# Second input projection: ten gate and query tiles as five pairs of seven half-size products, the third weight sum of pairs two to five on GpSimd

## What is computed

```python
h = _rms(x, norm_g) * (1.0 + scale) + shift
u = h @ w_in                       # 1024 x 1984
cq     = u[..., 0:256]             # query latent: 2 tiles of 128 columns
ckv    = u[..., 256:384]           # key/value latent: 1 tile
k_rope = u[..., 384:448]           # rotary keys: 1 tile, half used
gate_a = u[..., 448:960]           # gate of the attention branch: 4 tiles
pool_in = u[..., 960:1472]         # input of the pooling branch: 4 tiles
gate_p = u[..., 1472:1984]         # gate of the pooling branch: 4 tiles
q = (_rms(cq, q_lora_g) @ w_uq)
pooled = window_mean(pool_in) - pool_in        # windows 2, 4, 8, 16 of four groups
y_p = (pooled @ w_pool[group]) * pool_scale
br_a = silu(gate_a) * attention(q, k, v)
br_p = silu(gate_p) * y_p
out = x + gate * (concat(br_a, br_p) @ w_out)
```

## Time and profile before

| | us |
|---|---|
| median of 3 runs | 1904.95 |
| lowest and highest | 1904.12, 1905.85 |
| span of the profiled execution, from its first to its last instruction | 1904.2 |
| TensorE busy | 1864.6 |
| VectorE busy | 1397.6 |
| GpSimd busy | 906.7 |
| ScalarE busy | 733.7 |

### The profile page before, as it was taken

One profiled execution on the slowest core, in us unless ns is written; L12 is line 12 of the kernel. 1 busy time (PEld: TensorE's weight loads), 2 busy tenths in 40 slices (PEclk: granted clock), 3 DMA queues, 4 the chain that ended last, 5 costly groups with the idle time before them and its releaser, 6 DMA issues.

```text
span 1904.2 us, 23795 instructions
## 1 busy us (share of the span) xinstructions
PE 1864.6 (98%) x8807; PEld 1544.8 (81%) x8807; DVE 1397.6 (73%) x1423; ACT 733.7 (39%) x990; POOL 906.7 (48%) x632
## 2 busy tenths in 40 slices
PE   7999999999999999999999999999999999999998
PEld 6788888778888888888887788878788878888887
DVE  7989988667348889898989786574633846667683
ACT  5433344441225333333341200243433236766643
POOL 5866766533334555555566555332233521222462
PEclk9999999999999999999999999999999999999999
DMA  4112234356112323232336435111123210000052
GB/s 164 52 45 89 67 111 144 122 177 187 45 45 66 100 67 99 66 99 66 99 136 232 146 106 198 56 41 38 45 82 112 84 45 1 12 12 1 1 177 67
DMA packets 190952, 166.63 MB, mean 88 GB/s; under 512 B 11267, under 2 KB 168912, under 8 KB 190864
## 3 DMA queue, kind: packets, MB, share of 16 engines
q1 hardware_dynamic: 189536, 162.82, 27.0%
q10 hardware_dynamic: 1328, 2.60, 0.4%
HBM read 134.72 MB, written 30.41 MB: 87 GB/s over the span
## 4 chain that ended last, share of the span: by engine, by line
PE 84%; DVE 8%; ACT 3%; issue 2%; DMA 1%; POOL 1%; ACTq 0%; SPq 0%; DVEq 0%
PE ps L963 33%; PE ps L1251 19%; PE ps L1108 16%; PE ps L1638 3%; PE ps L1454 2%; PE ps L1489 1%; PE ps L1487 1%; PE ps L1488 1%; PE ps L1468 1%; PE ps L1465 1%; PE ps L1471 1%; PE ps L1474 1%; PE ps L1462 1%; DVE resid L2707 1%; DVE mod_acc L2410 1%
## 5 line engine op out<-in xcount | busy, mean ns | idle before, releaser
L833 POOL TENSOR_TENSOR small<-ones 128x1 f32<-128x1 f32 x75 | 22.2, 296 | 479.0 <-PE ps L963 438.7
L963 PE MATMUL ps<-xb_hi,whi 128*128 128x512 f32 x752 | 244.6, 393 | 5.1 <-DVE resid L2707 2.3
L963 PE MATMUL ps<-xb_lo,whi 128*128 128x512 f32 x752 | 242.2, 389 | 0.0
L963 PE MATMUL ps<-xb_hi,wlo 128*128 128x512 f32 x752 | 242.0, 389 | 0.0
L838 POOL TENSOR_TENSOR wlo<-raw,whi 128x1024 fp32r<-128x1024 f32 (+1 forms) x72 | 197.4, 2742 | 6.0
L879 POOL TENSOR_TENSOR wlo<-w_sums,whi 128x512 fp32r<-128x512 f32 x80 | 138.1, 1745 | 82.3 <-ACT whi L1956 82.3
L963 PEld LDWEIGHTS ps<-xb_hi,whi 128*128 128x128 f32 x752 | 140.2, 188 | 38.0 <-DVE resid L2707 3.1
L963 PEld LDWEIGHTS ps<-xb_lo,whi 128*128 128x128 f32 x752 | 141.2, 188 | 29.7 <-issue 0.2
L963 PEld LDWEIGHTS ps<-xb_hi,wlo 128*128 128x128 f32 x752 | 141.2, 188 | 29.6
L2390 DVE SCALAR_TENSOR_TENSOR ps<-glu_pad,tab,ps 128x1024 f32<-128x1024 f32 x116 | 149.2, 1286 | 2.9
L933 POOL TENSOR_SCALAR prob<-prob,small 128x512 f32<-128x512 f32 x64 | 50.5, 802 | 180.8 <-DVE small L3045 180.2
(11 more groups left out here) (493 smaller groups left out, 4824.6 us busy)
## 6 DMA issues: line engine op xcount, KB each, us to landing
t<-in_w_mod SPq DMA_DIRECT2D x48, 256.0 KB, 2.9
f_scratch<-t SPq DMA_DIRECT2D x22, 512.0 KB, 2.7
raw<-in_w_down SPq DMA_DIRECT2D x22, 512.0 KB, 4.2
raw<-in_w_up SPq DMA_DIRECT2D x40, 256.0 KB, 3.7
w_raw<-in_w_up SPq DMA_DIRECT2D x40, 256.0 KB, 3.7
raw<-in_w_in SPq DMA_DIRECT2D x18, 512.0 KB, 4.0
raw<-in_w_in SPq DMA_DIRECT2D x36, 256.0 KB, 4.0
w_in_raw<-in_w_in SPq DMA_DIRECT2D x32, 256.0 KB, 3.7
```

What stands on the lines that cost most here:

```text
L833: nc.gpsimd.tensor_tensor(small[:, 106 + slab.slot:107 + slab.slot], ones[:, 0:1], ones[:, 0:1], ALU.mult)
L963: ins = mm(dst[j], w, r[j], start=first and f, stop=last and l)
```

## The change

The ten tiles become five pairs (`UP_AT`, `u_product`): pair 0 the query tiles, 1 and 2 gate_a, 3 and 4 gate_p. The four combinations of h are made by four in-place subtractions on VectorE from a second, full copy of h (`hfull`, written by ScalarE beside the high part), then split in high (`comb_hi`) and low (`comb_low`). GpSimd makes the weight low halves and, for pairs 1 to 4, the third weight sum. The four pooling tiles now come right after the key tiles, the row sums stand in the first of them before k step 3, and the first two products with w_pool follow the second and third pooling tile, the other two stand between products of pair 0. Pooled outputs and Silu gates go through DRAM and come back for the products of gate and pooled output (`branch_gate`) and, before the first head's result, as `ga`. In the heads two branch tiles are split in place of one.

```diff
+NUP = 5
+UP_AT = {(0, 1): 0}
+for _p in range(NUP):
+    for _k in (2, 6, 5, 7):
+        UP_AT[_p, _k] = len(UP_AT)
+    if _p + 1 < NUP:
+        UP_AT[_p + 1, 1] = len(UP_AT)
+    for _k in (4, 3):
+        UP_AT[_p, _k] = len(UP_AT)
+UP_PRODUCTS = len(UP_AT)
...
+                for g in range(UP_PRODUCTS):
+                    slot, cols = u_ring(g)
+                    pool.wait_ge(*on("u_hi", g + 1))
+                    nc.gpsimd.tensor_tensor(wlo[:, slot, cols], u_source(*UP_OF[g]), f32(whi[:, slot, cols]),
+                                            ALU.subtract).then_inc(sem("u_split"), 1)
+                    p, k = UP_OF[g]
+                    if k == 3 and p + 1 < NUP:
+                        u_raw_in(pool, p + 1)
+                        pool.wait_ge(*on("u_split", g + 1))
+                        nc.gpsimd.tensor_tensor(u_sum(p + 1, 2), u_raw(p + 1, 0), u_raw(p + 1, 2), ALU.subtract).then_inc(sem("u_third"), 1)
+                pool.wait_ge(*on("u_done", UP_AT[4, 7] + 1))
                 head_split(0)
+                pool.wait_ge(*on("u_done", UP_PRODUCTS))
...
-        gemm(J + 4, L + 2, XBh, XBl, KD, w8)
-        gemm(J + 5, L + 3, XBh, XBl, KD, w8)
-
         def lora_sums(n):
 
-            if n == 2:
+            if n == 3:
                 pe.wait_ge(sem("y_ready"), 8)
                 row_sums(sqck, NKEY, sem("lora_sq"), 3)
...
+        def pooled_product(n):
+
+            gq = GROUPS[n]
+            pe.wait_ge(split_done, SLABS["w_pool"] + 2)
             pe.wait_ge(sem("branch2_lo"), n + 1)
-            gemm(J + (2 * n + 1), None, XAh[:, 4 + gq:5 + gq, :], XAl[:, 4 + gq:5 + gq, :], 1,
-                 lambda k: (gq, slice(0, P)), new_slab=False, weights=(wpoolh, wpooll))
+            if n:
+                pe.wait_ge(*on("wp_read", n))
+            else:
+                pe.wait_ge(sem("ck_f"), 1)
+            halves = [(PS[:, H * (6 + c):H * (7 + c)], slice(H * c, H * (c + 1))) for c in range(2)]
+            split_products([o for o, _ in halves], wpoolh[:, gq, :], wpooll[:, gq, :], [plh[:, 0, q] for _, q in halves],
+                           [pll[:, 0, q] for _, q in halves], True, True).then_inc(sem("wp_done"), 1)
+
+        J = Lin(JOBS["pin"])
+        L, LB = Lin(SLABS["pin"]), Lin(SLABS["pin_b"])
+        gemm(J, L, XBh, XBl, KD, w8, between=lora_sums)
+        gemm(J + 1, L + 1, XBh, XBl, KD, w8, begins=3)
+        pooled_product(0)
+        gemm(J + 2, LB, XBh, XBl, KD, w8)
+        pooled_product(1)
+        gemm(J + 3, LB + 1, XBh, XBl, KD, w8)
+
+        def u_product(p, k):
+
+            g, o = UP_AT[p, k], win_bank(p, k)
+            slot, cols = u_ring(g)
+            pe.wait_ge(*on("u_split", g + 1))
+            if p == 0 and k in HX:
+                pe.wait_ge(*on("hx_dve", 4 + HX_ORDER.index(k) + 1))
+            if (p, k) == (0, 5):
+                pe.wait_ge(pair_free[1], (J + 3).half() + 1)
+            if (p, k) == (1, 1):
+                pe.wait_ge(pair_free[0], (J + 2).half() + 1)
+            if k == 1 and p >= 2:
+                pe.wait_ge(*on("u_act", 3 * p - 5))
+            if k == 2 and p >= 2:
+                pe.wait_ge(*on("u_add", 3 * p - 5))
+            if k == 5 and p >= 2:
+                pe.wait_ge(*on("u_add", 3 * p - 3))
+            if k in (6, 7, 4):
+                pe.wait_ge(*on("u_copy", 3 * p + {6: 1, 7: 2, 4: 3}[k]))
+            if k == 3:
+                pe.wait_ge(*on("u_add", 3 * p + 2))
+            for j in range(4):
+                w = slice(cols.start + j * P, cols.start + (j + 1) * P)
+                if k in HX:
+                    b, k0, c0 = HX[k]
+                    bh, bl = xch[:, b, j, :], XAl[:, k0 + j, c0:c0 + H]
+                else:
+                    k0, c0 = {1: (0, 0), 2: (4, 0), 3: (4, H)}[k]
+                    bh, bl = XBh[:, k0 + j, c0:c0 + H], XBl[:, k0 + j, c0:c0 + H]
+                for i, (wp, bp) in enumerate(((whi, bh), (whi, bl), (wlo, bh))):
+                    last = mm(o, wp[:, slot, w], bp, start=k in (1, 2, 5) and j == 0 and i == 0,
+                              stop=j == 3 and i == 2, skip_group_check=True)
+            last.then_inc(sem("u_done"), 1)
+
+        for p, k in UP_AT:
+            u_product(p, k)
+            if (p, k) == (0, 1):
+                pooled_product(2)
+            if (p, k) == (0, 5):
+                pooled_product(3)
+            if (p, k) == (1, 7):
+                pe.wait_ge(*on("wp_read", 4))
+                column_sums(pres[0], 8, 16, sem("s12_done"), 23)
 
...
             fn(XBh[:, m, :], hT[:, m, :], ACT.Identity, bias=mod_sb[:, m, 0:1]).then_inc(sem("h_hi"), 1)
-        row_log(Q1, D, 6, 0, S, at_col=6 * H)
-        row_scale(PS[:, 6 * H:6 * H + S], Q1[:, :]).then_inc(sem("rbc_ready"), 1)
+            fn(hfull[:, m, :], hT[:, m, :], ACT.Identity, bias=mod_sb[:, m, 0:1]).then_inc(sem("h_hi"), 1)
+        row_log(rbc, D, 6, 0, S, at_col=6 * H)
+        row_scale(PS[:, 6 * H:6 * H + S], rbc[:, :]).then_inc(sem("rbc_ready"), 1)
+
+        def comb_hi(k):
+
+            b, k0, c0 = HX[k]
+            act.wait_ge(*on("hx_dve", HX_ORDER.index(k) + 1))
+            fn(xch[:, b, :, :], hfull[:, k0:k0 + 4, c0:c0 + H], ACT.Copy).then_inc(sem("hx_hi"), 1)
+
+        for k in HX_ORDER[:3]:
+            comb_hi(k)
         keys_out(J + 2, 0, S)
         rope_out(J + 3, 0, S)
...
+        def u_hi(g):
+
+            if g >= UP_PRODUCTS:
+                return
+            p, k = UP_OF[g]
+            slot, cols = u_ring(g)
...
+                act.wait_ge(*on("u_done", g - 1 if g == UP_PRODUCTS - 2 else g - 3))
+            if k in (1, 2, 4):
+                u_raw_in(act, p)
+            elif k == 7 and p:
+                act.wait_ge(sem("u_third"), p)
+            else:
+                act.wait_ge(*on("u_sum", up_sums(p, k)))
+            fn(whi[:, slot, cols], u_source(p, k), ACT.Copy).then_inc(sem("u_hi"), 1)
+
+        def u_copy(p, n):
+
+            k, to = ((1, upc[p % 2][:, 0:H]), (6, upc[p % 2][:, H:S]), (7, upd[p % 2][:, H:S]))[n]
...
+            act.wait_ge(*on("u_done", UP_AT[p, k] + 1))
+            fn(to, win_bank(p, k), ACT.Copy).then_inc(sem("u_copy"), 1)
...
+        def branch_high(p, n):
+
+            act.wait_ge(*on("u_dve", 2 * (p - 3) + n + 1))
+            act.wait_ge(*on("u_done", UP_AT[4, 5] + 1))
+            fn(XAh[:, 4 + GATE_P[p][1 - n], :], (upd, upc)[n][p % 2][:, :], ACT.Copy).then_inc(sem("branch2_hi"), 1)
...
+            if p == 0:
+                pooled_out(3)
+                comb_hi(4)
+            u_hi(b + 7)
+            if p + 1 < NUP:
+                u_copy(p + 1, 0)
+                u_hi(b + 8)
+                u_hi(b + 9)
+            else:
+                branch_high(3, 0)
+                branch_high(3, 1)
+            u_last_block(p)
+            u_hi(b + 10)
+            u_finish(p)
...
             if m >= 1:
-                dve.wait_ge(sem("h_hi"), m)
+                dve.wait_ge(sem("h_hi"), 2 * m)
                 dve.wait_ge(sem("h_n"), m)
                 stt(XBl[:, m - 1, :], hT[:, m - 1, :], mod_sb[:, m - 1, 0:1], f32(XBh[:, m - 1, :]),
                     ALU.add, ALU.subtract).then_inc(sem("h_lo"), 1)
-        dve.wait_ge(sem("lora_sq"), 6)
-        tt(cqs[:, 0, :], cqs[:, 0, :], cqs[:, 1, :], ALU.add).then_inc(sem("s12_done"), 1)
+        dve.wait_ge(sem("h_hi"), 16)
+        for n, (to, a, b) in enumerate((((0, 0), (0, H), (0, 0)), ((0, H), (4, H), (0, H)), ((4, H), (4, H), (0, 0)), ((4, 0), (4, 0), (4, H)))):
+            o, x, y = (hfull[:, k0:k0 + 4, c0:c0 + H] for k0, c0 in (to, a, b))
+            if n:
+                dve.wait_ge(*on("hx_dve", n))
+            tt(o, x, y, ALU.subtract).then_inc(sem("hx_dve"), 1)
         dve.wait_ge(sem("rbc_ready"), 5)
         for m in range(8):
             stt(R[:, m, :], R[:, m, :], col("g_final", m), PS[:, 6 * H:6 * H + S], ALU.mult, ALU.mult).then_inc(sem("y_ready"), 1)
 
+        def comb_low(k):
+
+            b, k0, c0 = HX[k]
+            dve.wait_ge(*on("hx_hi", HX_ORDER.index(k) + 1))
+            tt(XAl[:, k0:k0 + 4, c0:c0 + H], hfull[:, k0:k0 + 4, c0:c0 + H], f32(xch[:, b, :, :]), ALU.subtract).then_inc(sem("hx_dve"), 1)
+
+        for k in HX_ORDER[:3]:
+            comb_low(k)
         nc.vector.tensor_copy(onesr[:, :], ones[:, :]).then_inc(sem("ksq_ready"), 1)
-        dve.wait_ge(sem("ksq_hi"), 1)
-        tt(KSQ[ROPE:P, :], sqkr[:, :], f32(KSQ[0:ROPE, :]), ALU.subtract).then_inc(sem("ksq_ready"), 1)
         J = Lin(JOBS["mla_in"])
         dve.wait_ge(sem("y_out"), GOES_ON["y_out"][1] + 8 * 16)
-        for k in range(2):
...
+        for x in (upad, wA, wB):
+            nc.vector.memset(x[:, :], 0.0).then_inc(sem("pads2_zero"), 1)
         dve.wait_ge(*free(J + 3))
         dve.wait_ge(sem("rope_in"), 96)
-        tt(U3[0:ROPE, 0:S], U3[0:ROPE, 0:S], sinb[:, :], ALU.mult).then_inc(sem("krot_mul"), 1)
-        tt(krot[:, 0:S], krT[:, 0:S], cosb[:, :], ALU.mult).then_inc(sem("krot_done"), 1)
```

(8 more changed lines are left out.)

409 lines of the change are left out of this document (274 added, 135 removed).

## The result

The median of four runs is 1931.9 us (1930.6 to 1935.1) against 1905.4 us for the kernel before in the same session: 1.0140 times as long, 95% interval 1.0126 to 1.0155. The profiled execution took 1932.6 us, its span is 1930.8 us, 26.6 more than the span of the kernel before. The forecast was 1929 us, from a span 24.2 us longer.

The account below looks back on a forecast made before the run. TensorE, busy 98% of the span, was taken as the bound. Savings of 13.6 and 0.9 us against new waits, clock loss and other costs summed to +24.2 on 1904.2, 1928.4 in span, 1929 us as median; range 1916 to 1937.

Parts of the forecast that it names:

- What bounds, what is removed: Rewritten stretch: TensorE bounds, half-size products cost the same per matmul; 60 fewer give -13.6 us, the gate's Silu wait -0.9.
- Entry: Up to the end of the key tiles: double writing of h delays VectorE's low parts and TensorE, +1.1 us.
- First wait: First pooling tile: TensorE waits for VectorE's differences and g_final products before the row sums, +12.5 us; slab split, +1.4.
- Second wait: First pooled product, after the second pooling tile: TensorE waits for VectorE's low part of that group, +12.7 us.
- Pairs: Half-size products in steady state: GpSimd and ScalarE work hides, moved third sums cost 0; two places do not hide.
- Fourth combination: After product 7 of pair one: h's fourth combination is made late, so TensorE waits, +3.8 us.
- Last pair: End of the pairs: no next pair's product to put between, so bank copies are waited for, +2.0 us.
- Clock: Behind the waits: lower granted clock counts only after the second wait, +1.7 us.
- Head entry: First head: the last pair's final sum and Silu come first, two branch tiles are split, TensorE waits, +3.5 us.
- Rival 1: VectorE is ready when TensorE comes, at both waits and the fourth combination: 1897 us, faster; chance 0.06.
- Rival 2: Only the wait ahead of the row sums occurs, as pooling catches up: 1915 us; chance 0.12.
- Rival 3: More collisions of VectorE and GpSimd: 1937 us; chance 0.13.

Follow-up runs that it names:

- experiment 5: Changed kernel with the third weight sum of pairs two to five moved from GpSimd back to VectorE: 1931.7 us, ratio 1.0144.
- Experiment 1: Changed kernel with the row sums of the key latent moved from the first pooling tile to the second: 1931.1 us, ratio 1.0136.
- Experiments 1 to 4: Changed kernel with row sums a tile later (1931.1 us), g_final products ahead of three differences (1925.8), low parts behind pooled groups (1932.2), both of the last two (1920.2).
- experiment 6: Changed kernel with ScalarE making the high part of h's fourth combination before reading the last pooled output: 1928.2 us, ratio 1.0124.
- experiment 10: Changed kernel with many reorderings, pooled groups in order of one to four shifts: 1909.5 us; the same without the last group's four shifted adds: 1902.3 us.
- experiment 7: Changed kernel with two ScalarE steps reordered, latent-key high parts before rotary ones and product 6's copy before a weight half: 1929.3 us, ratio 1.0128.
- experiment 2: Changed kernel with g_final products after the first difference of h and ScalarE's latent and rotary key copies before the combinations' high parts: 1925.8 us, ratio 1.0107.

## Why the prediction was right, and where only its sum was

**What bounds, what is removed.** Right: half-size products cost the same per matmul. The 84 matmuls of a pair take 19.04 us (1524.11 to 1543.15, experiment 5), 0.2267 each.

**Entry**, +1.1: measured +0.9. VectorE's last low part, with the 0.7 us of the common part taken off, ended at 1388.3, 1.0 earlier than the 1389.3 of the sum.

**First wait**, 13.9 with the split: 9.4 measured. The first piece, 5.1 in place of 1.4, had a second cause that the sum lacked: the slab's low half came 3.5 us behind TensorE, not 1.4, and ScalarE's copy out of the bank, behind three high parts, 1.6 later still. That only divides the stop; its end is VectorE's eighth product with g_final, as the sum said. The step that was mis-sized is "four differences end at 1403.3". They met one GpSimd low half and not two, so that the eighth product came 21.6 us behind the last low part, not 23.6. Of the 4.5 that the term was too high this is 2.0; 0.9 are TensorE's later arrival, 6.5 us behind the last low part and not 5.6, and 1.5 are matmuls at the lower clock, which took what would else be wait. Experiment 1 shows that this size did not matter for the sum as long as the second stop comes behind it.

**Second wait**, +12.7: measured +13.4. Experiments 1 to 4 show that it is the whole list that ends there, with the store of y as a second bound at its middle, both of which the sum had. The length of the list, 56.0 us in the sum and 56.7 measured, owes something to luck, since two errors cancel: up to the eighth product it was 2.0 shorter than forecast, and behind it 2.7 longer (35.1 against 32.4). The store landed 1.0 later, the rotary steps took 1.0 more, the first shifted add beside GpSimd's split 2.0 more (3.27 us against 1.25), and the low part of the rotary squares was done 1.5 sooner.

**Pairs.** The moved third sum cost nothing (experiment 5), though for another reason than the rows that the sum read: beside it none of VectorE's sums was stretched. Fourth combination 3.8, measured 3.7; experiment 6 took off the 1.5 us of the steps put ahead of it. Last pair 2.0, measured 2.1.

**Clock**, +1.7: measured +7.6. I charged the lower clock once, behind the second wait. By TensorE's starts it cost 1.5 us behind the first stop (18 matmuls from 1400.52 to 1406.14, 5.6 us where 4.1 are due), 1.8 behind the row sums' stop, 2.7 behind the pooled product's (14 matmuls from 1445.67 to 1451.56, 5.9 for 3.2) and 1.5 behind the fourth combination's. The first two are paid by nobody: they make the next wait shorter by as much, as the prediction said of the first, and so they are missing from the two waits' measured sizes (10.9 and 15.2 with them, 26.1 together, where the sum had 26.6). What I left out is 1.0 behind the pooled product and 1.5 behind the fourth combination. The step that was mis-sized is "+1.7": in this execution a stop of 3.7 us brought the clock down too.

**Head entry**, +3.5: measured +3.4, and 349.8 to 351.7 us from the head to the end in the other traces, so 3.2 to 5.1.

**Rivals.** Rival 1 (VectorE hidden after all) is out by both waits; even in the version of experiment 10 that computes everything TensorE still stands 5.2 us for a low part of VectorE. Rival 2 (only the first wait) is out: the second was the longer one. Rival 3 (1937) stays outside the runs, 1930.6 to 1935.1.

## What to carry to other kernels

Where one engine works through a list and another meets it at several points, the waits must not be priced one by one: find the last point at which they meet, and ask how long the list is up to there and how much the other engine can do before it. A saving of matmuls that is paid for with element-wise steps on VectorE is worth nothing where VectorE has no time left: here 13.6 us of TensorE against eight steps of 2.3 us on VectorE, for the combinations of h alone. Beside a list, look for the second bound that lies just under it (the store of y), since it decides whether a single edit shows anything.

## What was not expected of the hardware

Behind every stop of TensorE of 3.7 to 13.4 us in the changed kernel matmuls ran at the lower granted clock, 0.50, for some 2.7 to 5.4 us, 7.6 us of time in all, while the kernel before, with 1.0 us idle in the stretch, has none; behind one wait of 3.7 us in experiment 5 and one of 3.5 us in experiment 7 it stayed at 1.00 (in the latter the six row sums took 2.42 us), and in experiment 2 it fell behind one of 2.1 us (the six row sums took 3.74 us). What tells these apart is open; it was not tried.

VectorE's steps that read PSUM kept their length beside GpSimd's steps, and GpSimd's theirs: the products with g_final took 1.2 us each and a slab's low half 2.41, and an addition from PSUM (L3307) took 0.69 beside the moved weight sum. Steps from SBUF to SBUF did not: the four differences took 12.2 us in place of 9.2, a shifted add 3.27 in place of 1.24, and the low half beside the differences 4.26.
